# More row slots and a larger TensorE share for block 0's expert sum in a retention, attention and expert layer

## The chip, the cores and the metric

One core of a Trainium2 chip runs the whole layer. The metric is the device time of one execution in microseconds; the time before is 1657.94 us, the median of three runs (1656.93 to 1660.45).

## The reference

One decoder layer on 512 tokens of 1024 floats, all in fp32. The tokens are four blocks of 128.

```python
proj = x @ w_in                                     # 7 groups of 512 columns
r = silu(rg) * group_norm(retention(rot(rq), rot(rk), rv))     # 4 heads
d = 0.8 * rms_norm((softmax(q1 k1) - lam * softmax(q2 k2)) v)   # 4 heads, causal
x = layer_norm(alpha * x + concat(r, d) @ w_out)
q = x @ w_query                                     # 8 heads, 2 halves
# per head: 16 best keys of each half, 16 best of their 256 sums
idx, gate = top_pairs(q, sub_keys)                  # 128 experts for each token
h = gelu(sum_d(x * U[idx]))                         # one dot product per expert
ffn = sum_e(gate * h * V[idx])                      # one weighted row per expert
x = layer_norm(alpha * x + ffn)
```

Each token needs 128 rows of U and 128 rows of V, 4 KB each. These gathers are 537 MB of the 603 MB that the core moves.

## The kernel before, in words

**Block 0 goes first.** It is projected, mixed and queried alone (WAVES[0]), up to about 126 us. Then its 128 U rows and 128 V rows are gathered and used while blocks 1 to 3 are projected, mixed and queried (WAVES[1]). One gather fills one slot: the same expert position for all 128 tokens, 128x1024 floats, 512 KB. Four make a group, so there are 32 U groups and 32 V groups (`HALVES`). U group k is used by VectorE in `dots(k)` (L1039, second input in PSUM, result into `hid`). V groups are summed in two ways: groups 0 to 7 (`ON_PE`) by TensorE in `add_rows(j)` (L461), as a product with a diagonal matrix of the weights that ScalarE builds in `diagonals(j)` (L870), accumulated in the PSUM tile ACC; groups 8 to 31 by VectorE in `sums(k)` (L1052, both inputs and the output in SBUF).

**The slots.** `ring` has eight slots (arena columns 14K to 18K), two groups. The list `ROWS` gives the order of the 64 groups: U 0 to 19, then V and U in turn, then the rest of V. GpSimd (POOL) issues them in this order (L438); before each slot it waits until the group two places earlier in the list has been used (`slot_used`).

**The pairs.** For blocks 1 to 3, one gather brings an expert's U and V row together, 1 MB: 384 pairs (L426) into 18 slots (`fused`, `NS`). Three pairs are issued behind V group 21 and three behind group 24 (`early`); pair 6 and the rest stand behind all rows in POOL's queue, and pair 6 also waits until the queries' key scores are stored (`keys_scored`), since pair slots 6 to 13 hold the query's operands. Pairs 14 to 17 go into the memory of the eight row slots. Pair 18 and each after it wait until TensorE has summed the pair 18 places earlier (L474). VectorE makes the pairs' dot products (L1060).

**The order of the engines is written out by hand.** In blocks 1 to 3, `attend(b, beside)` on TensorE does for each head: the scores of the next head (L661), which wait for this head's exponentials; the V groups named in `beside`; the transposes of this head's probabilities (L681), which wait for VectorE's `softmax_join`; the product with v (L685), which waits for ScalarE's copy. ScalarE's `attention` does exponentials (L880, after the transposes of the head before), the diagonals of `beside`, then the copy (L888). VectorE does `softmax_max`, `rows(1)` (one group, U or V, whichever is next), `softmax_join`. After the four heads come ScalarE's squares (L896), VectorE's `diff_norm` (L1243), and on TensorE `mixed_out`: transposes (L707, L725) and the output projection (L716). VectorE's `ln1(b)` (from L1252) waits for the projection. `ln1(3)` is followed by the queries on TensorE (L744, scores L754), and by `retrieve` on VectorE, which ends with the expert numbers (L1311) that the pairs wait for.

**Weights.** A row's weight needs gelu of `hid`. ScalarE's `gelu_0` and VectorE's `weights` do it for quarters of 32 experts: quarter 0 ahead of block 1's heads, quarters 1 to 3 in block 3's head 0.

Of the kernel before, what the change touches and what calls it, by code (L numbers as in the profile page):

```python
# [29 lines left out]
ALU = mybir.AluOpType  # L30
# [23 lines left out]
RING = 8  # L54
HALF = RING // 2

# [8 lines left out]
AT = {row: p for p, row in enumerate(ROWS)}  # L65

# [54 lines left out]

def tiles_before(b):

    return b * (b + 1) // 2


def ring_slots(p):

    return range(p % 2 * HALF, (p % 2 + 1) * HALF)


def landed(p):

    return 16 * (p // 2 + 1)


def used(p):

    return p // 2 + 1
# [8 lines left out]
def build(nc, x, xT, w_in, ret_gn_g, ret_gn_b, lq1, lk1, lq2, lk2, subln_g, w_out, ln1_g, ln1_b,  # L148
          w_query, keysT, uv, ln2_g, ln2_b, decay, rope, ident_in, mask_in, decay_far, out):
    ctx = ExitStack()  # L150
    with ctx:
# [18 lines left out]
        dqT = part(2 * K + 1536, 1536, "p (h t) -> p h t", h=H)  # L170
        swish = part(2 * K + 3072, 1536, "p (i n) -> p i n", i=3)
        gn = part(2 * K + 4608, 1536, "p (i n) -> p i n", i=3)
        work = part(5 * K, D)
        dec = part(5 * K + D, D, "p (c n) -> p c n", c=2)
        attn = part(6 * K, 1536)
        rp = part(6 * K + 1536, 512, "p (c b n) -> p c b n", c=2, b=NB)
# [3 lines left out]
        ring = part(14 * K, 4 * K, "p (r d) -> p r d", r=RING)  # L180
# [10 lines left out]
        rv = sb("rv", [P, NB, HW])  # L191
        dkT = sb("dkT", [P, H, S])
# [207 lines left out]
        def _(pool):  # L400
# [4 lines left out]
            early = {("V", 21): (0, 3), ("V", 24): (3, EARLY)}  # L405
# [6 lines left out]
            def pair(n):  # L412
# [4 lines left out]
                if n == 0:  # L417
                    pool.wait_ge(mixer_ready, 2 * NB)
                elif n == EARLY:
                    pool.wait_ge(keys_scored, 4 + 3 * WQ)  # L420
                elif LATE <= n < NS:
                    for r in (2 * (n - LATE), 2 * (n - LATE) + 1):
                        pool.wait_ge(slot_used[r], HALVES)
                elif n >= NS:
                    pool.wait_ge(pairs_summed, n - NS + 1)
# [5 lines left out]
            for p, (table, k) in enumerate(ROWS):  # L431
                if table == "U" and k * HALF % QUARTER == 0:
                    pool.wait_ge(experts_ready, k * HALF // QUARTER + 1)
                for m, r in enumerate(ring_slots(p)):
                    if p >= 2:
                        pool.wait_ge(slot_used[r], used(p - 2))
                    e = k * HALF + m
                    pool.indirect_dma_start(  # L438
                        out=ring[:, r, :], out_offset=None, in_=rows,
# [8 lines left out]
        def _(pe):  # L448
            fill = [0]

            def add_rows(j):

                p = AT["V", j]
                for m, r in enumerate(ring_slots(p)):
                    e = j * HALF + m
                    if e == 0:
                        pe.wait_ge(ret_decayed, tiles_before(NB))
                    pe.wait_ge(row_landed[r], landed(p))
                    pe.wait_ge(diag_ready, e + 1)
                    for half in range(2):  # L460
                        last = nc.tensor.matmul(  # L461
                            ACC[:, half * HW:(half + 1) * HW], fdiag[:, e % ND, :], ring[:, r, half * HW:(half + 1) * HW],
                            start=e == 0, stop=e == ON_PE * HALF - 1)
# [305 lines left out]
            attend(1, [[0], [1], [2], [3]])  # L769
            add_rows(4)  # L770
            mixed_out(1)
            attend(2, [[5], [6], [7], []])
            mixed_out(2)
            attend(3, [[], [], [], []])
# [7 lines left out]
        def _(act):  # L782
# [74 lines left out]
            def project_1():  # L857

                for f in FILLS[fill[0]:]:
                    take_fill(1, WAVES[1])  # L860

            def diagonals(j):

                for e in range(j * HALF, (j + 1) * HALF):
                    if e == 0:
                        act.wait_ge(weights_ready, 1)
                    if e >= ND:
                        r, count = slot_of("V", e - ND)
                        act.wait_ge(slot_used[r], count)
                    nc.scalar.activation(fdiag[:, e % ND, :], ident[:], ACT.Copy,  # L870
                                         scale=gate[:, e:e + 1]).then_inc(diag_ready, 1)

            def attention(b, beside):
                keys_n = (b + 1) * P
                for h in range(H):
# [9 lines left out]
                    if b == 3 and h == 0:  # L885
                        gelu_0(1, 4, 2)
# [592 lines left out]
```

## Time and profile before

| | us |
|---|---|
| device time, median of three runs | 1657.94 |
| span of the profiled execution | 1633.5 |
| outside the span (their difference) | 24.4 |
| TensorE, VectorE busy in the span | 1276.5, 1155.6 |
| ScalarE, GpSimd busy in the span | 267.2, 625.2 |

The profiled execution has no time of its own beside its span, so the span is set against the median. The page gives busy shares over the whole span; the span has stages with different limits, so it is read by stretches, and then along the timeline of each engine.

### The profile page before, as it was taken

How to read it: one execution, taken by the hardware profiler on the slowest of the kernel's cores; microseconds unless marked ns; L12 is line 12 of the kernel's file. 1: busy time of each engine (PE TensorE's matmuls, PEld its weight loads, DVE VectorE, ACT ScalarE, POOL GpSimd, SP SyncE). 2: the span in 40 equal slices, each digit the busy share in tenths (PEclk: the TensorE clock that was granted, in tenths of full speed). 3: DMA queues.
4: the chain of work that ended last, by engine and by line, in shares of the span. 5: the costliest groups of instructions: out<-in, count | busy, mean ns of one | idle time of the engine just before them, and what ended most of it. 6: DMA issues, size and time to landing. Idle time of an engine off the chain costs nothing.

```text
span 1633.5 us, 11511 instructions
## 1 busy us (share of the span) xinstructions
PE 1276.5 (78%) x3448; PEld 618.1 (38%) x3448; DVE 1155.6 (71%) x2727; ACT 267.2 (16%) x754; POOL 625.2 (38%) x645
## 2 busy tenths in 40 slices
PE   7879979888646994586978687878777878787885
PEld 5465446433323562232323233333333333332332
DVE  1349999767798979987676767776767677764454
ACT  0110000121211111121212121212121212121111
POOL 0004344474445565543434343434342434343320
PEclk9989999999767997798888888989897989899899
DMA  9939798897759898999999999999999999999993
GB/s 339 390 140 353 280 344 312 319 409 274 263 189 335 319 373 329 410 422 421 422 421 421 422 422 421 422 421 422 421 422 421 422 421 422 421 422 421 421 422 127
DMA packets 125710, 603.44 MB, mean 369 GB/s; under 512 B 12624, under 2 KB 14928, under 8 KB 76368
## 3 DMA queue, kind: packets, MB, share of 16 engines
q0 software_dynamic: 92160, 536.91, 81.2%
q1 hardware_dynamic: 33488, 65.80, 11.0%
q8 instruction: 27, 0.44, 0.1%
q14 instruction: 35, 0.29, 0.1%
HBM read 600.57 MB, written 2.10 MB: 369 GB/s over the span
## 4 chain that ended last, share of the span: by engine, by line
DMA 38%; PE 31%; DVE 23%; issue 3%; POOL 2%; SPq 1%; ACT 1%; DVEq 0%; POOLq 0%
DMA arena<-uv,idx 37%; PE W L474 7%; PE W L509 7%; DVE arena L1060 5%; PE ACC L474 4%; DVE xs L1052 4%; PE W L744 3%; PE W L716 3%; PE ACC L461 2%; POOL arena L438 2%; PE W L515 2%; DVE arena L1039 1%; DMA arena<-w_in 1%; DVE cand L1301 1%; DVE cand L1303 1%
## 5 line engine op out<-in xcount | busy, mean ns | idle before, releaser
L474 PE MATMUL W<-arena,fdiag 128*128 128x512 f32 x1024 | 498.9, 648 | 170.1 <-ACT fdiag L979 170.1
L426 POOL DMA_INDIRECT arena<-uv,idx x384 | 367.5, 957 | 586.7 <-PE W L474 355.7
L1060 DVE SCALAR_TENSOR_TENSOR arena<-arena,X 128x1024 f32<-128x1024 f32 x256 | 309.2, 1219 | 200.8 <-DMA arena<-uv,idx 199.7
L438 POOL DMA_INDIRECT arena<-uv,idx x256 | 257.3, 1005 | 372.2 <-DVE idx L1311 125.1
L474 PEld LDWEIGHTS W<-arena,fdiag 128*128 128x128 f32 x1024 | 208.6, 208 | 459.7 <-issue 253.0
L474 PE MATMUL ACC<-arena,fdiag 128*128 128x512 f32 x512 | 254.9, 660 | 69.3 <-ACT fdiag L979 69.3
L1060 DVE SCALAR_TENSOR_TENSOR arena<-arena,W 128x1024 f32<-128x1024 f32 x128 | 154.8, 1219 | 95.8 <-DMA arena<-uv,idx 95.4
L474 PEld LDWEIGHTS ACC<-arena,fdiag 128*128 128x128 f32 x512 | 107.0, 213 | 217.2 <-issue 132.1
L979 ACT ACTIVATE fdiag<-ident,gate 128x128 f32<-128x128 f32 x384 | 123.3, 390 | 354.7 <-DVE gate L1067 351.0
L1039 DVE SCALAR_TENSOR_TENSOR arena<-arena,X 128x1024 f32<-128x1024 f32 x128 | 150.0, 1216 | 24.8 <-DMA arena<-uv,idx 24.3
L509 PE MATMUL W<-arena 128*128 128x512 f32 x320 | 143.7, 605 | 9.7 <-DMA arena<-w_in 9.0
L1052 DVE SCALAR_TENSOR_TENSOR xs<-arena,gate,xs 128x1024 f32<-128x1024 f32 x96 | 123.3, 1284 | 19.3 <-DMA arena<-uv,idx 11.1
L744 PE MATMUL W<-arena 128*128 128x128 f32 (+1 forms) x512 | 116.8, 391 | 1.4 <-ACT arena L912 1.4
L971 ACT ACTIVATE hid<-hid 128x4 f32<-128x4 f32 x96 | 19.7, 205 | 456.5 <-DVE arena L1060 456.5
L744 PEld LDWEIGHTS W<-arena 128*128 128x128 f32 x512 | 80.2, 198 | 36.2 <-ACT arena L912 2.2
L509 PEld LDWEIGHTS W<-arena 128*128 128x128 f32 x320 | 60.8, 194 | 81.9 <-issue 76.9
L515 PE MATMUL W<-arena 128*128 128x128 f32 (+1 forms) x256 | 58.9, 388 | 10.8 <-DVE arena L1157 9.4
L461 PE MATMUL ACC<-arena,fdiag 128*128 128x512 f32 x128 | 59.0, 615 | 4.2 <-DMA arena<-uv,idx 4.2
L515 PEld LDWEIGHTS W<-arena 128*128 128x128 f32 x256 | 39.0, 194 | 28.4 <-issue 11.8
L716 PE MATMUL W<-arena 128*128 128x512 f32 x96 | 43.8, 616 | 0.7 <-ACT arena L912 0.7
L461 PEld LDWEIGHTS ACC<-arena,fdiag 128*128 128x128 f32 x128 | 24.5, 197 | 36.0 <-issue 29.7
L716 PEld LDWEIGHTS W<-arena 128*128 128x128 f32 x96 | 18.7, 198 | 25.1 <-issue 23.2
(178 smaller groups left out, 824.7 us busy)
## 6 DMA issues: line engine op xcount, KB each, us to landing
arena<-w_in SPq DMA_DIRECT2D x13, 2048.0 KB, 13.8
arena<-peer_w_query SPq DMA_DIRECT2D x8, 2048.0 KB, 14.4
arena<-uv,idx POOLq DMA_INDIRECT x640, 25.4
arena<-w_out SPq DMA_DIRECT2D x4, 2048.0 KB, 14.9
arena<-w_in SPq DMA_DIRECT2D x4, 512.0 KB, 6.4
out<-xs SPq DMA_DIRECT2D x4, 512.0 KB, 8.1
arena<-xT SPq DMA_DIRECT2D x1, 1536.0 KB, 18.2
xs<-x SPq DMA_DIRECT2D x1, 1536.0 KB, 17.0
```

Source lines behind the costliest of these rows:

```text
L426: pool.indirect_dma_start(out=fused[slot], out_offset=None, in_=uv, in_offset=bass.IndirectOffsetOnAxis(ap=idx[:, E + n:E + n + 1], axis=0 ...
L438: pool.indirect_dma_start(out=ring[:, r, :], out_offset=None, in_=rows, in_offset=bass.IndirectOffsetOnAxis(ap=idx[:, e:e + 1], axis=0), e ...
L461: last = nc.tensor.matmul(ACC[:, half * HW:(half + 1) * HW], fdiag[:, e % ND, :], ring[:, r, half * HW:(half + 1) * HW], start=e == 0, sto ...
L474: last = nc.tensor.matmul(sum_of(b)[:, half * HW:(half + 1) * HW], fdiag[:, n % ND, :], fused[n % NS][:, D + half * HW:D + (half + 1) * HW ...
L509: last = nc.tensor.matmul(bank, actT[:, k, part * P:(part + 1) * P], wts[slot][:, k, :], start=(k == 0), stop=(k == KD - 1))
L515: last = nc.tensor.matmul(bank[:, at:at + n_tok], wts[slot][:, k, h * P:(h + 1) * P], actT[:, k, toks], start=(k == 0), stop=(k == KD - 1))
L716: last = nc.tensor.matmul(W[:, 2 + half, :], mixT[:, k, :], wts[slot][:, k, :], start=(k == 0), stop=(k == KD - 1))
L744: last = nc.tensor.matmul(dst, wts[slot][:, k, i * P:(i + 1) * P], actT[:, k, toks], start=(k == 0), stop=(k == KD - 1))
L979: nc.scalar.activation(fdiag[:, n % ND, :], ident[:], ACT.Copy, scale=gate[:, E + n:E + n + 1]).then_inc(pair_diag_ready, 1)
L1039: STT(out=ring[:, r, :], in0=ring[:, r, :], scalar=1.0, in1=X[:], op0=ALU.mult, op1=ALU.mult, accum_out=hid[:, e:e + 1]).then_inc(slot_use ...
L1052: STT(out=xs[:, 0, :], in0=ring[:, r, :], scalar=gate[:, e:e + 1], in1=xs[:, 0, :], op0=ALU.mult, op1=ALU.add).then_inc(slot_used[r], 1)
L1060: STT(out=fused[slot][:, 0:D], in0=fused[slot][:, 0:D], scalar=1.0, in1=token_of(b), op0=ALU.mult, op1=ALU.mult, accum_out=hid[:, E + n:E ...
```

## The change

There are sixteen row slots. The eight new ones lie in memory that is free once blocks 1 to 3's retention products are done (kT, rv, parts of the arena); `QUAD_AT` gives each group of `ROWS` four slots, two sets of four in turn up to U group 19, four sets in turn for the next 30 groups, two again from V group 18. POOL waits for `ret_mixed` before V group 0. TensorE sums 18 V groups (`PE_GROUPS`): 0 to 9, 11, 13, 15, 17 beside attention, and 28 to 31 after the queries of blocks 1 to 3. VectorE sums the other 14. The table `BESIDE` puts groups 3 and 4 into head 3 of block 1, 8 and 9 into head 3 of block 2, and one group into each head of block 3. The weights come in three steps: quarters 0 and 1 before the last projection, quarter 2 in block 2's head 2 with the scaling `residual(0)`, quarter 3 in block 3's head 0. VectorE's `rows` calls are set anew. Three early pairs each stand behind V groups 25 and 28, not 21 and 24. Pair 0 waits for the last use of slots 12 to 15, and ScalarE's first scores of blocks 1 to 3 for that of slots 8 to 11.

```diff
-RING = 8
-HALF = RING // 2
+RING = 16
+HALF = 4
 FIRST_V = 20
-ON_PE = 8
+AFTER_QUERY = [28, 29, 30, 31]
+PE_GROUPS = list(range(10)) + [11, 13, 15, 17] + AFTER_QUERY
+DVE_GROUPS = [j for j in range(HALVES) if j not in PE_GROUPS]
+TURNS = 10
 ROWS = ([("U", k) for k in range(FIRST_V)]
-        + [row for j in range(ON_PE) for row in (("V", j), ("U", FIRST_V + j))]
-        + [("U", k) for k in range(FIRST_V + ON_PE, HALVES)] + [("V", k) for k in range(ON_PE, HALVES)])
+        + [row for j in range(TURNS) for row in (("V", j), ("U", FIRST_V + j))]
+        + [("U", k) for k in range(FIRST_V + TURNS, HALVES)] + [("V", k) for k in range(TURNS, HALVES)])
+WIDE_FROM, WIDE_TO = FIRST_V, AT["V", 18]
+def quads_of(p):
+    if p < WIDE_FROM:
+        return p % 2
+    if p < WIDE_TO:
+        return ((p - WIDE_FROM) + 2) % 4
+    return (p - WIDE_TO) % 2
+WEIGH_AT = [None, (2, 2), (3, 0)]
+BESIDE = {1: [[0], [1], [2], [3, 4]], 2: [[5], [6], [7], [8, 9]], 3: [[11], [13], [15], [17]]}
+WEIGH = [(0, 2), (2, 3), (3, 4)]
...
-            early = {("V", 21): (0, 3), ("V", 24): (3, EARLY)}
+            early = {("V", 25): (0, 3), ("V", 28): (3, EARLY)}
...
+                if p == WIDE_FROM:
+                    pool.wait_ge(ret_mixed, NB)
                 for m, r in enumerate(ring_slots(p)):
-                    if p >= 2:
-                        pool.wait_ge(slot_used[r], used(p - 2))
+                    if used(p) > 1:
+                        pool.wait_ge(slot_used[r], used(p) - 1)
...
             query(1, WAVES[1])
+            for j in AFTER_QUERY:
+                add_rows(j)
             for b in range(1, NB):
                 add_pairs(b)
...
                 for f in FILLS[fill[0]:]:
+                    if fill[0] == len(FILLS) - 1:
+                        gelu_0(0)
                     take_fill(1, WAVES[1])
...
             gate_exp(4)
             gate_exp(5)
+            for j in AFTER_QUERY:
+                diagonals(j)
...
                     if h:
                         softmax_max(b, h)
-                    if taken[0] < HALVES or h:
-                        rows(1)
+                    rows(1)
                     softmax_join(b, h)
-                    if b == 2 and h == 0:
-                        rows(1)
                     if b > 1 and h == 0:
                         ln1(b - 1)
-                    if b == 3 and h == 0:
-                        weights(1, 4, 2)
+                    if (b, h) == WEIGH_AT[1]:
+                        weights(1)
                         residual(0)
+                    if (b, h) == WEIGH_AT[2]:
+                        weights(2)
+                    if b == 2 and h % 2:
+                        rows(1)
                 rows(1)
                 diff_norm(b)
                 if b < NB - 1:
                     softmax_max(b + 1, 0)
                 if b == 2:
-                    rows(HALVES - taken[0])
-            rows(3)
-            ln1(3)
-            rows(5)
-            retrieve(1, 0)
-            rows(5)
-            retrieve(1, 1)
-            rows(2 * HALVES - ON_PE - taken[0])
+                    rows(max(0, HALVES - taken[0]))
+            rows(2)
+            ln1(3)
+            rows(4)
+            retrieve(1, 0)
+            rows(3)
+            retrieve(1, 1)
+            rows(HALVES + len(DVE_GROUPS) - taken[0])
```

## Rows read from the trace of the kernel before

**Rows 1.** Page: span, engines' busy time, GB/s in 40 slices, dots of block 0

```profile
span 1633.5 us, 11511 instructions
...
PE 1276.5 (78%) x3448; PEld 618.1 (38%) x3448; DVE 1155.6 (71%) x2727; ACT 267.2 (16%) x754; POOL 625.2 (38%) x645
...
GB/s 339 390 140 353 280 344 312 319 409 274 263 189 335 319 373 329 410 422 421 422 421 421 422 422 421 422 421 422 421 422 421 422 421 422 421 422 421 421 422 127
...
L1039 DVE SCALAR_TENSOR_TENSOR arena<-arena,X 128x1024 f32<-128x1024 f32 x128 | 150.0, 1216 | 24.8 <-DMA arena<-uv,idx 24.3
```

**Rows 2.** Busy time by stretch: PE, PEld, DVE, ACT, POOL; PE clock, DMA share, GB/s

```profile
300.00:460.00 160.00, 125.40 (x355) 59.55 (x353) 110.73 (x252) 36.30 (x109) 79.34 (x84) 0.91 0.82 307
...
460.00:500.00 40.00, 14.29 (x47) 9.13 (x48) 37.60 (x61) 7.28 (x23) 20.14 (x16) 0.50 0.58 193
...
627.00:655.00 28.00, 2.53 (x23) 2.33 (x21) 25.91 (x21) 3.31 (x6) 21.90 (x21) 0.62 0.91 332
...
700.00:1590.00 890.00, 700.99 (x1422) 293.58 (x1421) 597.57 (x1441) 162.40 (x478) 334.94 (x353) 0.89 1.01 422
```

**Rows 3.** Timeline of POOL: start, duration, line, what, [idle before <- releaser]

```profile
316.59 0.94 POOL L438 DMA_INDIRECT arena<-uv,idx  x1 [17.46 <-DVE arena L1039]
...
319.07 0.94 POOL L438 DMA_INDIRECT arena<-uv,idx  x1 [0.30 <-issue]
...
386.97 0.93 POOL L438 DMA_INDIRECT arena<-uv,idx  x1 [0.78 <-PE ACC L461]
...
388.69 0.94 POOL L438 DMA_INDIRECT arena<-uv,idx  x1 [0.79 <-PE ACC L461]
...
571.73 1.73 POOL L426 DMA_INDIRECT arena<-uv,idx  x1 [14.77 <-DVE idx L1311]
...
626.38 1.93 POOL L438 DMA_INDIRECT arena<-uv,idx  x1 [15.12 <-DVE xs L1052]
...
628.62 1.08 POOL L438 DMA_INDIRECT arena<-uv,idx  x1 [0.30 <-issue]
...
655.00 1.08 POOL L426 DMA_INDIRECT arena<-uv,idx  x1 [0.30 <-issue]
```

**Rows 4.** Timeline of PE, 300 to 630 us: V rows, attention, output, queries

```profile
317.46 8.23 PE L461 MATMUL ACC<-arena,fdiag 128*128 128x512 f32 x16
...
348.39 7.13 PE L461 MATMUL ACC<-arena,fdiag 128*128 128x512 f32 x16 [1.70 <-DMA arena<-uv,idx]
...
365.60 1.04 PE L707 MATMUL W<-ident,arena 128*128 128x128 f32 x8
...
434.93 1.97 PE L707 MATMUL W<-ident,arena 128*128 128x128 f32 x8 [5.19 <-DVE arena L1243]
...
439.89 14.00 PE L716 MATMUL W<-arena 128*128 128x512 f32 x32
...
453.82 1.13 PE L661 MATMUL W<-dkT,arena 64*128 64x512 f32 x4
...
466.82 2.08 PE L661 MATMUL W<-dkT,arena 64*128 64x512 f32 x4 [9.06 <-ACT arena L880]
...
499.37 1.97 PE L707 MATMUL W<-ident,arena 128*128 128x128 f32 x8 [4.93 <-DVE arena L1243]
...
503.73 15.82 PE L716 MATMUL W<-arena 128*128 128x512 f32 x32 [0.69 <-ACT arena L912]
...
626.52 3.00 PE L754 MATMUL W<-arena 128*128 128x128 f32 x24 [0.58 <-ACT arena L929]
```

**Rows 5.** Timeline of DVE: the end of block 1's norm

```profile
360.87 1.13 DVE L1243 SCALAR_TENSOR_TENSOR arena<-W,rstd,arena 128x128 f32<-128x128 f32 x4
```

**Rows 6.** Timeline of ACT: table load and exponential in block 3, gates after the queries

```profile
456.57 1.28 ACT L880 ACT_TABLE_LOAD   x1
...
474.32 0.69 ACT L880 ACTIVATE arena<-W,nmax 128x512 f32<-128x512 f32 x1
...
630.06 0.34 ACT L965 ACTIVATE gate<-gate 128x32 f32<-128x32 f32 x2
```

More of the change, by code:

```diff
@@ L127, in ring_slots, with used, uses_of, weighed_by @@
 def ring_slots(p):
-    return range(p % 2 * HALF, (p % 2 + 1) * HALF)
+    return range(QUAD_AT[p] * HALF, (QUAD_AT[p] + 1) * HALF)
+def used(p):
+    return QUAD_AT[:p + 1].count(QUAD_AT[p])
 def landed(p):
-    return 16 * (p // 2 + 1)
-def used(p):
-    return p // 2 + 1
+    return 16 * used(p)
+def uses_of(quad):
+    return QUAD_AT.count(quad)
+WEIGH = [(0, 2), (2, 3), (3, 4)]
+def weighed_by(j):
+    return [n for n, (lo, hi) in enumerate(WEIGH) if lo <= j * HALF // QUARTER < hi][0] + 1
 def slot_of(table, e):
@@ L169, in build @@
         qT = part(2 * K, 1536, "p (h t) -> p h t", h=H)
[L170 to L176, printed above, removed]
+        rp = part(2 * K + 1536, 512, "p (c b n) -> p c b n", c=2, b=NB)
+        dqT = part(3 * K, 1536, "p (h t) -> p h t", h=H)
+        swish = part(3 * K + 1536, 1536, "p (i n) -> p i n", i=3)
+        work = part(3 * K + 3072, D)
+        dec = part(5 * K, D, "p (c n) -> p c n", c=2)
+        gn = part(5 * K + D, 1536, "p (i n) -> p i n", i=3)
+        attn = part(6 * K + 512, 1536)
         keys = part(7 * K, K, "p (c n) -> p c n", c=HC)
@@ L191, in build @@
         rv = sb("rv", [P, NB, HW])
+        kT_flat = kT[:].rearrange("p h n -> p (h n)")
+        rv_flat = rv[:].rearrange("p b n -> p (b n)")
+        ring = ([part(14 * K + r * D, D) for r in range(8)]
+                + [kT_flat[:, 0:D], kT_flat[:, D:2 * D], rv_flat[:, 0:D], rv_flat[:, D:2 * D]]
+                + [part(2 * K, D), part(2 * K + D, D), part(5 * K, D), part(D, D)])
         dkT = sb("dkT", [P, H, S])
@@ L418, in pair @@
                     pool.wait_ge(mixer_ready, 2 * NB)
+                    for r in range(12, RING):
+                        pool.wait_ge(slot_used[r], uses_of(3))
                 elif n == EARLY:
@@ L934, in query @@
                             act.wait_ge(keys_scored, m + 1)
+                            if w and s == 0 and j == 0:
+                                for r in range(8, 12):
+                                    act.wait_ge(slot_used[r], uses_of(2))
                             nc.scalar.activation(scores[b][:, s * HW:(s + 1) * HW], W[:, m % 2, :],
@@ L950, in token_to_psum, with gelu_0 @@
                 last.then_inc(token_in_psum, 1)
-            def gelu_0(lo, hi, call):
+            def gelu_0(call):
+                lo, hi = WEIGH[call]
                 cols = slice(lo * QUARTER, hi * QUARTER)
@@ L1075, in gate_norm, with weights @@
                 link(TT(out=g, in0=g, in1=gsum[:, 0:2].unsqueeze(2).to_broadcast([P, 2, TOPK]), op=ALU.mult))
-            def weights(lo, hi, calls):
+            def weights(call):
+                lo, hi = WEIGH[call]
+                calls = call + 1
                 cols = slice(lo * QUARTER, hi * QUARTER)
@@ L1118, in join_sums @@
                 if b == 0:
-                    for r, count in (slot_of("V", E - 1), slot_of("V", ON_PE * HALF - 1)):
+                    for r, count in (slot_of("V", DVE_GROUPS[-1] * HALF + HALF - 1),
+                                     slot_of("V", PE_GROUPS[-1] * HALF + HALF - 1)):
                         dve.wait_ge(slot_used[r], count)
@@ L1352, in rows @@
                     else:
-                        sums(k - HALVES + ON_PE)
+                        sums(DVE_GROUPS[k - HALVES])
                 taken[0] += n
@@ L1377, in _ @@
                 retention_norm(b)
-            weights(0, 1, 1)
+            weights(0)
             softmax_max(1, 0)
```

63 lines of the change are left out of this document (33 added, 30 removed).

## The prediction

> **What bounds the kernel now.** I read the page first: neither TensorE (78% busy) nor VectorE (71%) fills the span, but from slice 18 on the DMA moves 421 to 422 GB/s in every slice but the last [rows 1]. The table by stretch says the same: 422 GB/s from 700 to 1590 us, with VectorE busy 598 us of 890 [rows 2]. In that tail only bytes count. The timeline of POOL shows where it begins: pair 6 is issued at 655.00, and behind it all is determined by the 378 pairs left, so the span ends 978.5 us later (1633.5 - 655.0). **The question is thus when pair 6 is issued.** It needs two things: the queries of blocks 1 to 3 (TensorE's last key product ends at 626.52 + 3.00 = 629.5, which I call Q [rows 4]), and the 64 groups of block 0 ahead of it in POOL's queue.
>
> Before, it is the queue that is late. POOL stands 15.12 us, to 626.38, for a slot that VectorE frees only after its retrieval, then issues the last 20 rows, one each 1.39 us (1.08 + 0.30), and pair 6 follows at 655.0, 25.5 us after Q [rows 3]. The bytes in the stretches 300 to 460 (307 GB/s) and 460 to 500 (193 GB/s) show much idle DMA time, and 460 to 500 is VectorE's: busy 37.6 us of 40, TensorE only 14.3 [rows 2]. It is tempting to price the change by that idle DMA time. But bytes moved earlier shorten the span only if pair 6 comes earlier, and this has the floor Q.
>
> **The change, part by part.** (1) *The end of the queue.* At Q only V groups 30 and 31, 8 rows, remain ahead of pair 6: by list order pairs 3 to 5 and group 29 need only group 27's slots, which VectorE frees ahead of its second retrieval. Group 30 takes the slots of group 28, and 31 those of 29, and TensorE uses these after the queries. ScalarE's gate exponentials end 0.9 us after Q (630.06 + 0.34 [rows 6]); one diagonal later, about Q + 1.3, group 28 starts. A row on TensorE takes 1.72 us, as the spacing of POOL's issues shows where TensorE frees the slots (386.97 to 388.69 [rows 3]), so the first of the 8 issues comes near Q + 3.5, the eighth 7 x 1.72 = 12.0 later, and pair 6 one issue (1.24) behind, at Q + 16.8. For Q = 629.5 that is 646.3, or 8.7 us earlier. Bounds: 1.24 us per issue if the slots were free (Q + 13.4), and 2.06 if each row took what the slow group took (8.23 for four [rows 4]; Q + 19.2).
>
> What is queued behind these rows? On TensorE the pairs' sums: groups 28 to 31 hold it 4 x 6.9 = 27.6 us, to about Q + 29. Pair 18 needs pair 0's sum, at Q + 31. Pairs 6 to 17 are 12 MB, 30 us at 422 GB/s, so the DMA has work to Q + 47. Then TensorE needs 1.72 us per pair against the DMA's 2.49, and catches up. This costs nothing, with 16 us of cover. Nor do pairs 14 to 17 wait long for the slots of groups 30 and 31. VectorE has fewer rows (56 against 96 at 1.39, 55 us less), all of it ahead of Q or in slack.
>
> (2) *Q itself moves*, since TensorE now does 6 more groups inside the chain that leads to the queries. I walk this chain by blocks; shifts are against the trace.
> Block 1: weights 0 come before the last projection, so head 0 starts 1.1 us earlier (before, gelu, its table load and four small VectorE instructions stood there). The slots let V1 and U20 be fetched in the 17.46 us in which POOL stood [rows 3], so TensorE's wait of 1.70 for rows [rows 4] and one of 0.8 go. Against that, group 4 moves from behind the last head, where it covered the squares and the norm, to ahead of that head's transposes. Before: group 3 starts at 348.39 and L707 at 365.60. After: group 3 at about 345.3, two groups (13.8 to 14.0) to 359.3, then transposes, product, squares and norm, 6.6 us (348.39 + 7.13 = 355.5 to the norm's end at 360.87 + 1.13 = 362.0 [rows 5]), so L707 at 365.9: **+0.3**.
> Block 2: the second U group of head 1 (4 x 1.2 on VectorE [rows 1], then the next maximum) holds head 2's exponentials to 405.9; group 7 ends at 413.9; transposes and copy 1.0, a table load of 1.28, since gelu of quarter 2 now stands there (as in the row at 456.57 [rows 6]), exponentials and a diagonal 1.7, groups 8 and 9 14.0, and 6.9 as above: L707 at 438.8 against 434.93: **+3.9**.
> Block 3: L707 to the output projection as before (434.93 to 439.89, and 14.00 long), so the heads start at 457.7. Group 11 hides in the 9.06 us that TensorE waited [rows 4]; the table load that lay in that wait now follows it, and head 2's scores start at 470.1 against 466.82: +3.3. A head with a group is then a chain on TensorE and ScalarE: scores 1.13 [rows 4], rows 6.9, transposes and copy 1.2, two exponentials of 0.69 with what follows each 1.45 [rows 6], 0.1 to 0.3 between: 10.9 us, where VectorE alone had set 9.0. Two heads, then the last group, 7.0 and 7.2 for the rest: L707 at 506.3 against 499.37, **+6.9**. The last projection took 15.82 where it takes 14.00 at full clock [rows 4]; with a busier TensorE ahead of it I give back 1.4: **+5.5**. From there, norm, queries (about 100 us of TensorE without a gap over 1 us) and their scores are unchanged, so Q is 635.0. The row supply stays ahead of this: 4.97 us per group of issues against heads of 9 to 11 us that use two, with slots for four.
>
> (3) *Nothing or near it:* POOL's wait for `ret_mixed` (3 us late for V0, but V0 is used 17 us later), the waits for slots 8 to 15 (last used in block 3's heads, needed 50 us later), and the early pairs behind group 25, which stand from about 552 to 578 for the same retrieval that held them 14.77 us before [rows 3]; the DMA is idle there, but the floor Q isn't touched.
>
> Sum: pair 6 at 635.0 + 16.8 = 651.8, 3.2 us earlier; I take 3. Span 1630.5, and with the 24.4 us between the profiled span and the median of the runs **1655 us**.
>
> [...] While VectorE sums V rows, POOL's issues come each 1.39 us, with dots running each 1.24 (0.94 + 0.30) [rows 3]: the same step as VectorE's own instruction. [...]
>
> **The rivals.** A: *the groups fit in TensorE's waits, Q stays within 3 us of 629.5.* For: TensorE was 64% idle in 460 to 500 [rows 2]. Against: the waits are for VectorE in one head and the group must fit into each of them. Price: pair 6 at 646.3, 8.7 earlier, 1649.2 us; 0.22.
> B: *the added groups run at the lower clock, and it is slower.* In 460 to 500 the granted clock was 0.50, 1.2 GHz, and 64x512 scores took 2.08 against 1.13 [rows 2, 4]. Each of the four instructions per row then takes twice 0.43, a group 13.8. If so for groups 13, 15 and 17, Q moves 3 x 6.9 = 20.7 more, pair 6 comes at 672.5, 17.5 later: 1675.4. It decides from the first group that is slow (3.2 of gain against 6.9). Against: the clock was 0.91 over 300 to 460, where groups stood beside the heads, and groups there took 7.13. 0.10. The Trainium skill, TensorE: Matmul & The Clock Gate, on oscillation in real kernels, tells of kernels whose TensorE runs cold because each wait throttles it again, which would give B; the trace shows this for sparse heads and not for heads with groups.
> C: *the chain is longer than I walked it*, Q moves 8 to 14: a head waits for rows that fall together with the 2 MB weight loads, or diagonals and table loads add up. Pair 6 at 654.3 to 660.3: -0.7 to +5.3, 1657 to 1663; 0.18. The sixteen slots bring nothing then. Forecast, Q moves 3 to 8, -6 to -0.5: 0.50.
>
> **How the numbers follow.** 0.2%, 3.3 us, is about what a measurement can tell from no change. Faster: all of A and 0.22 of the forecast's case, 0.44. Same: 0.28 of it and 0.10 of C, 0.38. Slower: B and 0.08 of C, 0.18. The range goes from A less 2 us, 1647, over the bounds of Q + 13.4 to Q + 19.2, to C's end, 1663; beyond are B and an A with a shorter chain.
>
> **What would show it.** In the changed kernel: L707 of block 3 at 506 and L744 near 535 to 536; rows of V groups beside block 3's heads at 7 us with a granted clock near 1.0; the eight last row issues 1.72 apart, starting 3.5 us after the last L754; pair 6 near 652 and the span's end 978 later; 422 GB/s from there on without a dip near Q + 47. A Q below 632 shows A, groups of 13 us B. The prediction is wrong at its root if the span's end doesn't follow pair 6, for instance if TensorE's late start leaves pairs waiting.

## The result: 12 us slower, and the profile after

The changed kernel takes 1669.56 us (four executions, 1668.45 to 1671.28) where the kernel before takes 1657.43 beside it: the ratio is 1.0082, with a 95% interval of 1.0063 to 1.0101. The forecast was 3 us faster. These lines are from the page of the changed kernel; they answer [rows 1]. L1091 is now the dots of block 0, L503 `add_rows`, L479 POOL's row issues, L465 its pair issues, L749 and L758 `mixed_out` (transposes and projection), L1300 `diff_norm`.

```profile
span 1667.9 us, 11861 instructions
...
PE 1356.7 (81%) x3608; PEld 653.0 (39%) x3608; DVE 1104.6 (66%) x2691; ACT 282.7 (17%) x798; POOL 619.3 (37%) x645
...
GB/s 341 389 122 331 275 335 318 317 407 220 325 298 296 277 194 361 261 423 421 422 421 422 421 422 421 422 421 422 421 422 421 422 421 422 422 421 422 421 421 133
...
L503 PE MATMUL ACC<-arena,fdiag 128*128 128x512 f32 x208 | 95.0, 613 | 2.4 <-ACT fdiag L916 1.3
```

VectorE has 51 us less to do and TensorE 80 more, as planned, and from slice 17 on the DMA moves 421 to 423 GB/s again. So the loss lies before the tail. The end of POOL's row queue comes next; it answers [rows 3]. Columns here and in all timelines: start, duration, engine and line, what, [idle before <- releaser].

```profile
676.13 0.94 POOL L479 DMA_INDIRECT arena<-uv,idx  x1 [25.27 <-PE ACC L503]
677.85 0.94 POOL L479 DMA_INDIRECT arena<-uv,idx  x1 [0.78 <-PE ACC L503]
...
688.15 0.94 POOL L479 DMA_INDIRECT arena<-uv,idx  x1 [0.78 <-PE ACC L503]
689.39 0.94 POOL L465 DMA_INDIRECT arena<-uv,idx  x1 [0.30 <-issue]
```

And this is TensorE around Q, the end of the queries' last key product, in the same execution [rows 4]:

```profile
669.60 3.00 PE L796 MATMUL W<-arena 128*128 128x128 f32 x24 [0.58 <-ACT arena L977]
673.90 27.71 PE L503 MATMUL ACC<-arena,fdiag 128*128 128x512 f32 x64 [1.30 <-ACT fdiag L916]
```

Q is 672.6. The first of the eight last rows is issued 3.5 us later, they are 1.72 apart, pair 6 follows at 689.39, which is Q + 16.8, and the span ends 978.5 behind it (1667.9 - 689.39). The tail is thus as forecast, to the tenth. **The whole error is Q: 672.6, where 635.0 was forecast and 629.5 was before.**

Where does Q lose 43 us? The timelines of ScalarE and VectorE show something that the profile of before does not have. Lines of the changed kernel:

```profile
136.60 0.60 ACT L977 ACTIVATE arena<-W 128x512 f32<-128x512 f32 x1 [10.66 <-remote]
...
260.65 0.49 ACT L870 ACTIVATE arena<-W 128x384 f32<-128x384 f32 x1 [10.51 <-remote]
...
380.05 0.28 ACT L944 ACTIVATE arena<-W 128x128 f32<-128x128 f32 x1 [3.16 <-issue]
...
381.22 0.17 DVE L1297 TENSOR_SCALAR rstd<-ssq 128x4 f32<-128x4 f32 x1 [14.49 <-issue]
...
476.96 0.43 DVE L1260 TENSOR_TENSOR W<-W,mask 128x256 f32<-128x256 f32 x1 [10.80 <-remote]
```

In all five rows the profile finds no releaser and writes "issue" or "remote". That alone doesn't make a row late; the distance to what it needs does. At 380.05, ScalarE's squares start 3.11 us after the start of the product they read (376.94). In an execution without such gaps (e2 below) it is 0.75 (358.30 to 359.05). At 136.60 ScalarE has stood 10.66 us where it stands 6.55 in e2, so it is 4.1 late, and at 476.96 VectorE begins 6.3 us after the end of the scores that it needs (TensorE, 469.54 + 1.13). The row at 381.22 is not late itself: ScalarE's read of the last square in front of it ends at 381.19. I call the others **late starts**. Between 100 us and Q, 23 waits of over 0.8 us on ScalarE, VectorE and GpSimd have no releaser, 14 of them on ScalarE; they hold the ordinary waits too, so neither their number nor their length is the loss.

In three places two engines begin again almost together after such a wait: VectorE at 260.40 and ScalarE at 260.65, ScalarE at 476.90 and VectorE at 476.96 in this trace, ScalarE at 385.51 and GpSimd at 385.63 in that of e14. That looks like one cause for both, but no run shows it.

### The profile page after: what moved, and what is told of

Its sections match the earlier page's. It is cut to its first block, busy times and chain, and to the rows that moved or that the text cites. A ratio compares the mean times of both kernels' runs of the same rounds, so it can differ in the third digit from the quotient of the medians.

```text
span 1667.9 us, 11861 instructions
## 1 busy us (share of the span) xinstructions
PE 1356.7 (81%) x3608; PEld 653.0 (39%) x3608; DVE 1104.6 (66%) x2691; ACT 282.7 (17%) x798; POOL 619.3 (37%) x645
## 4 chain that ended last, share of the span: by engine, by line
PE 41%; DMA 37%; DVE 13%; issue 4%; ACT 2%; another core or an unknown queue 1%; SPq 1%; POOL 0%; POOLq 0%; DVEq 0%; ACTq 0%
DMA arena<-uv,idx 36%; PE W L516 7%; PE ACC L503 7%; PE W L786 7%; PE W L551 7%; PE ACC L516 3%; DVE arena L1114 3%; PE W L758 3%; PE W L557 2%; DVE arena L1091 1%; PE W L796 1%; DMA arena<-w_in 1%; PE W L629 1%; PE W L687 1%
## 5 line engine op out<-in xcount | busy, mean ns | idle before, releaser
L465 POOL DMA_INDIRECT arena<-uv,idx x384 | 368.3, 959 | 598.4 <-PE W L516 356.5
L1114 DVE SCALAR_TENSOR_TENSOR arena<-arena,X 128x1024 f32<-128x1024 f32 x256 | 309.8, 1220 | 210.2 <-DMA arena<-uv,idx 209.4
L479 POOL DMA_INDIRECT arena<-uv,idx x224 | 219.4, 979 | 379.2 <-DVE idx L1368 124.0
L516 PE MATMUL ACC<-arena,fdiag 128*128 128x512 f32 x512 | 253.9, 658 | 69.8 <-ACT fdiag L1031 69.8
L516 PEld LDWEIGHTS ACC<-arena,fdiag 128*128 128x128 f32 x512 | 106.7, 212 | 217.0 <-issue 131.8
L551 PE MATMUL W<-arena 128*128 128x512 f32 x320 | 145.6, 611 | 8.8 <-DMA arena<-w_in 8.1
L1091 DVE SCALAR_TENSOR_TENSOR arena<-arena,X 128x1024 f32<-128x1024 f32 x124 | 143.8, 1216 | 3.5 <-issue 2.2
L786 PE MATMUL W<-arena 128*128 128x128 f32 (+1 forms) x512 | 118.1, 394 | 1.7 <-ACT arena L960 1.4
L503 PE MATMUL ACC<-arena,fdiag 128*128 128x512 f32 x208 | 95.0, 613 | 2.4 <-ACT fdiag L916 1.3
L786 PEld LDWEIGHTS W<-arena 128*128 128x128 f32 x512 | 80.9, 200 | 36.6 <-issue 2.7
L551 PEld LDWEIGHTS W<-arena 128*128 128x128 f32 x320 | 61.6, 197 | 82.1 <-issue 78.2
L1106 DVE SCALAR_TENSOR_TENSOR xs<-arena,gate,xs 128x1024 f32<-128x1024 f32 x48 | 61.6, 1284 | 21.0 <-DMA arena<-uv,idx 17.4
L557 PE MATMUL W<-arena 128*128 128x128 f32 (+1 forms) x256 | 61.6, 400 | 8.3 <-DVE arena L1214 8.3
L503 PEld LDWEIGHTS ACC<-arena,fdiag 128*128 128x128 f32 x208 | 40.1, 196 | 55.0 <-issue 55.0
L758 PE MATMUL W<-arena 128*128 128x512 f32 x96 | 46.4, 645 | 7.6 <-ACT arena L960 7.6
L557 PEld LDWEIGHTS W<-arena 128*128 128x128 f32 x256 | 40.5, 200 | 26.8 <-issue 13.2
L758 PEld LDWEIGHTS W<-arena 128*128 128x128 f32 x96 | 19.6, 208 | 34.2 <-issue 25.4
## 6 DMA issues: line engine op xcount, KB each, us to landing
xs<-x SPq DMA_DIRECT2D x1, 1536.0 KB, 17.1
```

What stands on the lines that cost most here:

```text
L465: pool.indirect_dma_start(out=fused[slot], out_offset=None, in_=uv, in_offset=bass.IndirectOffsetOnAxis(ap=idx[:, E + n:E + n + 1], axis=0 ...
L479: pool.indirect_dma_start(out=ring[r], out_offset=None, in_=rows, in_offset=bass.IndirectOffsetOnAxis(ap=idx[:, e:e + 1], axis=0), element ...
L503: last = nc.tensor.matmul(ACC[:, half * HW:(half + 1) * HW], fdiag[:, i % ND, :], ring[r][:, half * HW:(half + 1) * HW], start=i == 0, sto ...
L516: last = nc.tensor.matmul(sum_of(b)[:, half * HW:(half + 1) * HW], fdiag[:, n % ND, :], fused[n % NS][:, D + half * HW:D + (half + 1) * HW ...
L551: last = nc.tensor.matmul(bank, actT[:, k, part * P:(part + 1) * P], wts[slot][:, k, :], start=(k == 0), stop=(k == KD - 1))
L557: last = nc.tensor.matmul(bank[:, at:at + n_tok], wts[slot][:, k, h * P:(h + 1) * P], actT[:, k, toks], start=(k == 0), stop=(k == KD - 1))
```

## The experiments

Each kernel was run beside the kernel before on the same chip; the chips are not all alike, and that is half of the answer. In the table, Q and pair 6 are from the profiled execution.

| run | us | before beside it | ratio (95%) | Q | pair 6 | late starts |
|---|---|---|---|---|---|---|
| before, the profile shown | | | | 629.5 | 655.0 | none |
| after, on record | 1669.6 | 1657.4 | 1.0082 (1.0063 to 1.0101) | 672.6 | 689.4 | yes |
| e1 before | 1636.3 | 1637.3 | 0.9995 (0.9981 to 1.0010) | 628.5 | 654.3 | none |
| e2 after | 1639.6 | 1637.3 | 1.0007 (0.9994 to 1.0020) | 640.5 | 657.3 | none |
| e3 | 1626.2 | 1637.3 | 0.9939 (0.9917 to 0.9961) | 639.1 | 643.4 | none |
| e4 | 1635.7 | 1637.3 | 0.9992 (0.9978 to 1.0006) | 639.3 | 656.1 | none |
| e5 | 1626.2 | 1638.6 | 0.9922 (0.9892 to 0.9951) | 630.8 | 647.6 | none |
| e6 | 1615.6 | 1638.6 | 0.9860 (0.9834 to 0.9886) | 627.9 | 632.3 | none |
| e7 | 1660.2 | 1638.6 | 1.0130 (1.0103 to 1.0158) | 661.5 | 678.3 | none |
| e8 after | 1639.6 | 1638.6 | 1.0010 (0.9994 to 1.0026) | 639.9 | 656.7 | none |
| e9 before | 1656.0 | 1654.4 | 1.0012 (0.9997 to 1.0027) | 646.0 | 671.4 | yes |
| e10 after | 1670.4 | 1654.4 | 1.0092 (1.0062 to 1.0122) | 671.5 | 688.3 | yes |
| e11 (= e6) | 1647.5 | 1654.4 | 0.9952 (0.9932 to 0.9972) | 661.8 | 665.2 | yes |
| e12 (= e7) | 1658.8 | 1639.0 | 1.0118 (1.0100 to 1.0137) | 662.8 | 679.6 | none |
| e13 (= e7) | 1673.6 | 1654.6 | 1.0104 (1.0073 to 1.0134) | 676.3 | 693.1 | yes |
| e14 | 1665.0 | 1654.6 | 1.0059 (1.0039 to 1.0078) | 666.2 | 683.0 | yes |

### e1 and e2: both kernels again, unchanged

> The kernel before, unchanged. In the changed kernel's trace the tail went as forecast (pair 6 at 689.39, 16.8 us after the queries' end Q at 672.6; the span ends 978.5 us after it), but Q lies 43.1 us later than in the trace of before, of which 14.4 us are there when block 1's attention begins, in code that the change hardly touches, beside gaps with no releaser in the program (issue, remote). Theory S: the trace of before was of an execution without such gaps, and its usual executions have them. Then this trace has a span near 1655, Q near 651, and gaps that sum up to some 20 us. Theory C: the gaps come with the change. Then this trace has the span 1633 to 1636, Q at 629 to 631, and no such gaps.

> The changed kernel, unchanged. Both theories: about 1669.5 us, 12 slower than before, Q near 672, pair 6 near 689. If the gaps (issue, remote) stand at the same instructions as in the first trace, they belong to the program; if at others, to the execution.

The kernel before takes 1637 here, by e1 and by the runs beside it, and its profile is the one shown ahead of the prediction (span 1633.6 against 1633.5). The changed kernel takes 1639.62, not the 1669 that I expected in both theories: 2.3 us more than before, within what can be told apart. In its trace no engine stands over 1.0 us without a releaser between 100 and 660 us. So the late starts do not come with the change (e9 below shows them in the kernel before), and 12 us slower became "the same". In the timed executions of these runs the device time is 1.7 to 3.0 us longer than the span, and mostly 1.8. So the "24.4 us outside the span" of the prediction is no time that a single execution spends outside its span: the profile of before came from an execution without late starts, and its three times (1656.93 to 1660.45) lie where before is with them (e9, 1656.0).

The trace of e2 is the one to set the forecast against, since both profiles are then free of late starts. TensorE, end of block 1:

```profile
350.58 3.60 PE L503 MATMUL ACC<-kT,fdiag 128*128 128x512 f32 x8
354.01 3.60 PE L503 MATMUL ACC<-rv,fdiag 128*128 128x512 f32 x8
357.44 0.38 PE L723 MATMUL W<-ident,arena 128*128 128x128 f32 x2
358.30 0.71 PE L727 MATMUL W<-arena 128*128 128x128 f32 x4 [0.47 <-ACT arena L936]
363.90 1.97 PE L749 MATMUL W<-ident,arena 128*128 128x128 f32 x8 [4.89 <-DVE arena L1300]
366.55 1.65 PE L703 MATMUL W<-dkT,arena 64*128 64x384 f32 x4 [0.69 <-ACT arena L952]
368.13 15.87 PE L758 MATMUL W<-arena 128*128 128x512 f32 x32
```

Group 4 now stands ahead of the head's transposes (L723) and product (L727), so TensorE has nothing to do while the squares and `diff_norm` are made: it stands 4.89 us. The transposes behind that wait take 1.97 where they took 1.04, and the projection 15.87 where it took 14.00 (365.60 to 382.22 before for both, 16.6 us; 363.90 to 384.00 now, 20.1). Blocks 2 and 3 have the same wait, 4.77 us each. The granted clock (the column behind the five busy times; the last is GB/s) says why, in e2:

```profile
351.00:359.00 8.00, 7.53 (x22) 3.47 (x20) 0.00 (x0) 0.38 (x1) 6.17 (x7) 1.00 1.03 410
364.00:368.00 4.00, 3.31 (x12) 1.97 (x12) 0.00 (x0) 1.19 (x2) 0.07 (x1) 0.50 1.02 409
368.00:372.00 4.00, 4.00 (x7) 1.81 (x6) 3.68 (x6) 2.09 (x8) 0.72 (x1) 0.51 1.01 404
372.00:384.00 12.00, 12.00 (x30) 5.04 (x29) 3.76 (x10) 0.31 (x2) 3.11 (x4) 1.00 0.54 183
```

It is 1.00 (2.4 GHz) ahead of the wait, 0.50 (1.2 GHz) for the transposes and the first 4 us of the projection, and 1.00 again after that.

How much such a wait costs is not the same in each execution. The last projection stands behind a wait of 4.8 to 4.9 us in both kernels; here it is in e1 and in e2:

```profile
503.50 14.00 PE L716 MATMUL W<-arena 128*128 128x512 f32 x32 [0.69 <-ACT arena L912]
...
513.71 16.47 PE L758 MATMUL W<-arena 128*128 128x512 f32 x32 [0.69 <-ACT arena L960]
```

It took 15.82 in the profile of before and 14.00 in e1, which is the same kernel, and 16.47, 16.55 and 14.00 in e2, e8 and e3. So up to 2.5 us of a single trace's Q are chance. Block 1's projection, behind its new wait, is slow in all of e2, e3, e4 and e8 (15.2 to 16.3).

### e3 and e4: the last 16 rows, and block 3's heads

> Changed kernel, but V groups 28 to 31 are summed by VectorE behind its second retrieval and not by TensorE behind the queries. Theory T (the last rows wait for TensorE after the queries and cost 15 us there): rows 30 and 31 are issued before Q, pair 6 at Q + 1 to Q + 3 in place of Q + 16.8, so 13 to 15 us faster than the changed kernel: 1654 to 1657. Rival: VectorE is as late as in the kernel before (25.5 us after Q) and nothing is gained or it is slower: 1669 to 1678.

```diff
-AFTER_QUERY = [28, 29, 30, 31]
+AFTER_QUERY = []
```

13.5 us faster than e2, as expected, with Q as good as unchanged (639.1): pair 6 is issued 4.3 us after Q (Q + 1 to Q + 3 was expected) and not 16.8, as TensorE's four groups are no longer ahead of it. **The part of the change that puts 16 rows behind the queries costs 12.5 us of path**, even though the forecast counted its end, Q + 16.8, as a gain over Q + 25.5. Both are true: against the old order it is better, against VectorE doing the same rows in the new order it is worse.

> Changed kernel, but V groups 11, 13, 15, 17 are summed by VectorE, so that block 3's heads have no rows on TensorE. Theory W (the rows beside block 3's heads lengthen the chain): Q comes 5 to 8 us earlier; VectorE has 22 us more to do, behind its second retrieval, which may hold groups 28 and 29 to about Q: 1662 to 1668. Rival G (Q is late because of gaps of no releaser, not of rows): Q moves by less than 3 us or at random, 1668 to 1675.

```diff
-PE_GROUPS = list(range(10)) + [11, 13, 15, 17] + AFTER_QUERY
-BESIDE = {1: [[0], [1], [2], [3, 4]], 2: [[5], [6], [7], [8, 9]], 3: [[11], [13], [15], [17]]}
+PE_GROUPS = list(range(10)) + AFTER_QUERY
+BESIDE = {1: [[0], [1], [2], [3, 4]], 2: [[5], [6], [7], [8, 9]], 3: [[], [], [], []]}
```

Four groups less beside block 3's heads move Q by 1.2 and the time by 3.9. Theory W, which took the whole shift of 6.9 for block 3's, misses. Rival G has the size right, but not the reason, as there are no late starts here. Q alone misleads, though. The transposes behind the norms of blocks 2 and 3 in e4:

```profile
444.42 1.97 PE L749 MATMUL W<-ident,arena 128*128 128x128 f32 x8 [4.78 <-DVE arena L1300]
...
508.22 1.97 PE L749 MATMUL W<-ident,arena 128*128 128x128 f32 x8 [4.94 <-DVE arena L1300]
```

From one to the other it is 63.8 us, and 67.1 in e2 (442.29 to 509.35): the four groups cost 3.3 us of the path. The walk had put 3.0 there (the shift grows from 3.9 to 6.9), so this step held. The traces differ by nearly as much ahead of it: e4 reaches block 2's transposes 2.1 later than e2, with the same program up to there. Without the groups the last projection is no faster (16.43 against 16.47).

### e5 and e6: the last group moved behind the head

> Changed kernel, but in each of blocks 1 to 3 the last V group (4, 9, 17) stands behind the last head's product, beside squares and norm, as group 4 did before the change. In the changed kernel's trace on the chip of the last runs TensorE waits 4.8 to 4.9 us for the norm in each block, and after it the transposes take 1.97 in place of 1.04, the first projection 15.87 in place of 14.00, the last 16.47. Theory N (the uncovered norm and the lower clock behind it carry most of Q's shift of 11 us): three times 4.8 and some 4 us of clock, Q 12 to 18 us earlier, pair 6 still at Q + 16.8, so 12 to 18 us faster than the changed kernel beside it and 0.989 to 0.994 of the kernel before. Rival H (the heads' own length carries it): the group's 7 us come back elsewhere, less than 4 us faster.

```diff
-BESIDE = {1: [[0], [1], [2], [3, 4]], 2: [[5], [6], [7], [8, 9]], 3: [[11], [13], [15], [17]]}
+BESIDE = {1: [[0], [1], [2], [3]], 2: [[5], [6], [7], [8]], 3: [[11], [13], [15], []]}
+BEHIND = {1: 4, 2: 9, 3: 17}
...
+            add_rows(BEHIND[b])      # TensorE, behind attend(b)
...
+            diagonals(BEHIND[b])     # ScalarE, behind attention(b)
```

13.4 us faster than e2 and e8 (ratio to before 0.9922). The same stretch of TensorE as above, in e5 (L504 is `add_rows`, L750 and L759 `mixed_out`):

```profile
353.24 0.71 PE L728 MATMUL W<-arena 128*128 128x128 f32 x4 [0.47 <-ACT arena L940]
355.57 3.67 PE L504 MATMUL ACC<-kT,fdiag 128*128 128x512 f32 x8 [1.61 <-ACT fdiag L920]
359.07 3.60 PE L504 MATMUL ACC<-rv,fdiag 128*128 128x512 f32 x8
362.51 1.04 PE L750 MATMUL W<-ident,arena 128*128 128x128 f32 x8
364.28 0.92 PE L704 MATMUL W<-dkT,arena 64*128 64x384 f32 x4 [0.74 <-ACT arena L956]
365.13 14.00 PE L759 MATMUL W<-arena 128*128 128x512 f32 x32
```

The same two half-groups now lie in the wait; the transposes follow without a gap at 1.04 us, the projection takes 14.00. Its end is 379.13, 4.9 earlier, in block 1 alone. Q is 630.8, 9.1 to 9.7 earlier, with the same groups on the same engines. So what a group costs depends on its place. By the ends of the projections, blocks 1 and 2 give 4.9 and 4.7 us and block 3 nothing (379.13, 451.90, 521.73 against 384.00, 461.50, 530.18). There head 3 has no group now, TensorE stands more ahead of group 17, and that one runs in part at the lower clock (0.50 from 495 to 499):

```profile
495.12 10.02 PE L504 MATMUL ACC<-arena,fdiag 128*128 128x512 f32 x16 [1.61 <-ACT fdiag L920]
```

The 13.4 us are between medians; the profiled executions are 10.4 apart (1638.34 and 1627.94), which is the path.

> As the last one, and V groups 28 to 31 on VectorE, behind its second retrieval, as in e3 (which was 13 us faster than the changed kernel). If the two parts are independent the gains add: 25 to 31 us faster than the changed kernel, 0.981 to 0.986 of before. If VectorE becomes the one that is late (in e3 pair 6 came 4.3 us after Q, with row issues that waited for VectorE), only 17 to 24 us.

Both edits together: 1615.58, ratio 0.986 (0.9834 to 0.9886), the best version. The sum of the two alone would be 26.9 below e2, it is 24.0. At pair 6 nothing of the sum is missing: e3 and e5 move it by 13.9 and 9.7 us against e2, e6 by 25.0. In e6, as in e3, the tail behind it is 2 us longer than in e2 (981.1 and 980.9 against 979.1); why is open. POOL's timeline of e6:

```profile
620.35 1.93 POOL L480 DMA_INDIRECT arena<-uv,idx  x1 [15.06 <-DVE xs L1113]
622.58 1.09 POOL L480 DMA_INDIRECT arena<-uv,idx  x1 [0.30 <-issue]
...
632.30 1.09 POOL L466 DMA_INDIRECT arena<-uv,idx  x1 [0.30 <-issue]
```

With Q at 627.9 it is again the queue that is late, by VectorE's retrieval, the picture of [rows 3] with 8 rows behind it in place of 20.

### e7 and e12: only eight slots

> Changed kernel with the division of work and the order of the rows as changed, but only eight row slots in use; the two waits for the last use of slots 8 to 15 go, since these are not used. Theory R (the slots are what lets the rows keep ahead): heads wait for rows, Q 8 to 30 us later. Rival: the slots bring nothing, since a head of 9 to 11 us uses two groups and their issue takes 9.9: within 4 us of the changed kernel.

```diff
 def quads_of(p):
-    if p < WIDE_FROM:
-        return p % 2
-    if p < WIDE_TO:
-        return ((p - WIDE_FROM) + 2) % 4
-    return (p - WIDE_TO) % 2
+    return p % 2
```

(with the waits for the last use of slots 8 to 15 gone as well). 20.6 us slower than e8, Q 21.6 later. TensorE's timeline of e7, same stretch, `add_rows` at L497:

```profile
335.48 10.19 PE L497 MATMUL ACC<-arena,fdiag 128*128 128x512 f32 x16 [1.48 <-DMA arena<-uv,idx]
...
359.04 8.66 PE L497 MATMUL ACC<-arena,fdiag 128*128 128x512 f32 x16 [4.28 <-DMA arena<-uv,idx]
```

TensorE waits for rows in front of a group, and behind such waits the groups take 10.19 and 8.66 us in place of 7.13, at the lower clock (0.50 from 335.5 to 339 us, 0.61 from 359 to 363). With this division of the sum the sixteen slots are what carries it.

> Changed kernel with eight row slots in use, to be read on a chip where the late starts occur (before at 1650 to 1660 beside it). There the queries' end Q was 17.4 us later in the kernel before (628.5 to 646.0), but 31.6 us later in the changed one (639.9 to 671.5) and 33.9 in the variant with groups behind the heads. Theory D (twice as many row transfers in flight make the late starts more or longer): with eight slots Q goes from 661.5 on a quiet chip to 675 to 682, by 14 to 20. Rival K (the chain through ScalarE has less cover, whatever the slots): by 28 to 36, Q at 690 to 697. On a quiet chip (before at 1633 to 1641) both give Q 661 and 1660 us, and it tells nothing.

This one was meant for a chip with late starts and met one without: the time is that of e7.

### e8 to e11 and e13: the same kernels where engines start late

> The changed kernel once more, beside these. On the chip of the last runs it was 2.3 us slower than before (1639.6 against 1637.3) and had no gaps without a releaser; in the first measurement, 12.1 us slower (1669.6 against 1657.4), ScalarE started late at some ten places, 1 to 6 us each. If these gaps come from the chip and not from the run, this one gives about 1639 and a trace without gaps if it is on that chip, or 1665 to 1672 with gaps, and before at 1655 to 1660, if it is on one like the first.

A second chip without late starts: 1639.60, as e2.

> The kernel before, unchanged, to catch the condition of the first measurement (before 1657.4, changed 1669.6), whose changed trace has about 32 us of late starts of ScalarE with no releaser in the program. Theory P (the condition is one of the place where a kernel runs and delays every program): if it holds here, before is at 1655 to 1660 and its trace has such gaps of some 20 us in sum ahead of pair 6; if not, 1633 to 1640 without gaps.

> The changed kernel beside it. Under the condition: 1666 to 1672 with 25 to 35 us of gaps, since its chain leaves ScalarE less cover; without it 1637 to 1641, no gaps.

Here before takes 1656.0 and after 1670.4, ratio 1.0092: the result on record is there again. In e9 the kernel **before** has late starts too, the first in the same place as the changed kernel's:

```profile
136.94 0.60 ACT L929 ACTIVATE arena<-W 128x512 f32<-128x512 f32 x1 [10.59 <-remote]
```

So the condition is no property of the changed kernel alone. But its price is: before, Q moves from 628.5 to 646.0 (+17.4), after, from 639.9 to 671.5 (+31.6).

> The variant with the last group of a block behind its heads and groups 28 to 31 on VectorE. Without the condition 1614 to 1617, 0.986 of before, as before. Under it: pair 6 in this variant waits for the queries and for VectorE's rows, so 20 to 30 us of gaps on ScalarE move it by as much: 1636 to 1646, still faster than before beside it.

The best version loses 33.9 at Q (627.9 to 661.8) and 31.9 of time, and is still ahead of before, 0.9952 (0.9932 to 0.9972).

> As e12, which fell on a quiet chip. Where the late starts occur (before at 1650 to 1660 beside it), theory D (more transfers in flight make the late starts): Q from 661.5 to 675 to 682; rival K (less cover on the chain): Q at 690 to 697. Quiet: 661 and 1660 us, no answer.

The changed kernel with eight slots loses 13.5 to 14.8 at Q (661.5 and 662.8 to 676.3, where theory D expected 675 to 682 and rival K 690 to 697) and 14 of time, by one trace and two executions. The surplus of some 14 us over the kernel before (31.6 - 17.4) thus goes with the sixteen slots, and not with the new order or the larger share of TensorE, which e13 has as well. Without late starts the slots gain 20.6 (e7 against e8), with them only 3.2 (e13 against e10, on two chips), which the intervals of the two ratios don't tell from nothing.

### e14: one block's norm covered, with late starts

> Changed kernel, but V group 4 alone stands behind block 1's last head, beside squares and norm; blocks 2 and 3 as changed. In the changed kernel the wait for this norm is 4.9 us, and from the transposes to the projection's end it takes 20.1 us against 16.6 before, at the lower clock. If wait and clock are both given back: 7 to 9 us faster than the changed kernel. If only the wait: 4 to 5. If the rest of the chain absorbs it: under 2.

```diff
-BESIDE = {1: [[0], [1], [2], [3, 4]], 2: [[5], [6], [7], [8, 9]], 3: [[11], [13], [15], [17]]}
+BESIDE = {1: [[0], [1], [2], [3]], 2: [[5], [6], [7], [8, 9]], 3: [[11], [13], [15], [17]]}
...
+            add_rows(4)              # TensorE, behind attend(1)
...
+            diagonals(4)             # ScalarE, behind attention(1)
```

5.4 us faster than e10 (on another chip, with before at 1654.6 and 1654.4 beside them), Q 5.3 earlier, between the two sizes expected. TensorE in e14:

```profile
378.81 1.04 PE L749 MATMUL W<-ident,arena 128*128 128x128 f32 x8
386.65 1.65 PE L703 MATMUL W<-dkT,arena 64*128 64x384 f32 x4 [6.81 <-ACT arena L953]
```

The wait for the norm is gone and L749 comes 6.4 earlier than in e10 (378.81 against 385.22), but then ScalarE's copy is late, TensorE stands 6.81, and the scores run at 1.65 again. Covering one wait doesn't remove the late starts, they turn up at the next dependence.

## Why the prediction failed, by its own steps

**The end of the queue (step 1) held.** Q + 3.5, seven steps of 1.72 and Q + 16.8 are as forecast in e2 (640.5, 644.00, 657.26) and on record. The 978.5 from there to the end came out exactly on record and as 979.1 in e2; over all traces it is 978.4 to 982.4. The pairs behind the four groups cost nothing: `add_rows` took 27.71 of the forecast 27.6, and the DMA did not dip behind it.

**The walk to Q (step 2) was too short by half, without any late start.** It gave +5.5, e2 shows +11.0 against the 629.5 it started from (+11.9 against e1). Point by point, forecast and e2: first L707 (now L749) 365.9 and 363.9, second 438.8 and 442.3, third 506.3 and 509.35, end of the last projection 525.1 (506.3 + 20.2 - 1.4) and 530.2. The waits for the norm were in the walk (6.6 to 6.9 per block); what it left out is **what such a wait does to the clock behind it**. Block 1's transposes and projection take 20.1 where I kept 16.6, +3.5. I had assumed in the last block that a busier TensorE would give back 1.4 of the 15.82 of [rows 4], and it took 16.47: with the rest of that stretch +2.1. Block 2's heads took 2.0 more than walked, and that is the clock too: behind a wait of 2.53 us group 7 took 9.23 in place of 7.13, at clock 0.50 from 408 to 412. The other terms are within 0.8 and block 1 was 2.0 better than walked. These sum to the 5.5 that are missing (3.5 + 2.1 + 2.0 - 2.0 and small terms). Only the first is in each trace of this order; the 2.1 are 0 in e3, and block 1's gain is chance in part (its transposes begin at 362.6 in e8 and 367.2 in e3, with the same program up to there). The rows were there to be read: in [rows 4] L707 takes 1.04 in block 1, behind groups, and 1.97 in block 3, behind a wait of 4.93, with 15.82 for the projection after it. The change puts block 1 into that case, and I kept its 1.04 and 14.00. (Block 2 is no counterexample: its projection takes 14.00 in both kernels, since the transposes of x and the scores stand between and take the slow stretch.) In rival B I had asked whether the clock would slow the added groups; groups 13, 15 and 17 took about 7.1 each in e2, and it was group 7 and the product behind the norm that were slowed. The Trainium skill, TensorE: Matmul & The Clock Gate, section HAM oscillation — how this bites in real kernels, describes this for a wait on a DMA: the wait lets the clock down, and the products that follow pay for it. The trace agrees for a wait on VectorE: 15.87 us, with clock 0.51 in the first 4 us, behind the wait, 14.00 and 1.00 without it (e2, e5).

With the true Q, step 3's sum would have been pair 6 at 640.5 + 16.8 = 657.3, 2.3 later than before, and that is what e2 measured (+2.3 us, not clear of noise): rival C's case, to which I gave 0.18.

**The conversion to device time was wrong.** I took 1657.94 - 1633.5 = 24.4 us as lying outside the span; it is about 2 (1.7 to 3.0). That number was the sign that profile and times came from different conditions. Forecast faster or slower didn't depend on it as long as both kernels lose the same, which leads to the last point.

**The sign on record was decided by a term the prediction did not have.** Late starts add 17.1 us to the kernel before (1637.3 to 1654.4) and 30.8 to the changed one (1639.6 to 1670.4). 2.3 + 30.8 - 17.1 = 16.0, the distance of e10 to the kernel before; on record it is 12.1, with before at 1657.4. Against the forecast it adds up so: the span on record is 37.4 us longer than forecast (1667.9 against 1630.5), 5.5 by the walk and 32.1 by late starts (Q of 672.6 against e2's 640.5). The device time is only 14.6 longer (1669.6 against 1655), as 24.4 us had been added where 1.8 belonged. That two large errors cancelled in part is luck. That this surplus goes with the sixteen slots is what e13 and e7 show. How it comes about is argued only: with the slots, TensorE's and ScalarE's steps follow each other with less wait for rows in between, so a late start is less often hidden in one. The number of transfers in flight could also make each late start longer; no run separates the two. What makes an engine start late at all is open. Places come again (136.60 and 136.94 in two kernels, the block times of after on record and of e10 agree within 1.1 us), and by the times of before it is the chip that decides: 1650.7 to 1661.4 in all its executions on two chips, 1632.4 to 1644.0 in all on three others.

**What was right beside that:** the slots matter only through Q, bytes moved early shorten nothing (from 460 to 500 us the DMA of e2 moves 310 GB/s where before it moved 193 [rows 2], and the time is the same). VectorE's smaller share (51 us less busy) was off the path: e3 gives it 16 rows back and is faster. That the waits for slots 8 to 15 and for `ret_mixed` cost nothing is not tested, as no run leaves out these alone.

## What to carry to other kernels

When work is moved to another engine, ask where in its chain it lies relative to the waits it used to fill: one group per block, in front of a head and not behind it, cost 9 to 10 us of the path to Q and 10 of the profiled span (13 between medians), with the same work done by the same engines. A wait on TensorE is to be priced with the slower products behind it, read from the same instruction behind a wait and without one, in more than one trace, since the same 32 products behind the same wait took 14.00 to 16.55. And before a profile is used to the microsecond, its span should be set against the timed runs: a gap of 24 us where others show 2 means that the profile doesn't show the condition in which the times are taken.

## What the hardware showed that I had not expected

Late starts: on some chips an instruction begins up to 6 us after its last dependence (2.4 at 380.05 of the changed kernel, 6.1 in e14's row at 386.65, against 0.74 in e5), several of them at the same places from run to run and with no releaser in the trace, on ScalarE, VectorE and GpSimd. They cost 17 us of 1637 in one kernel, 31 to 32 in two with sixteen row slots, 13 to 15 in the changed kernel cut to eight. A change of 20 us on one chip (the slots, e7 against e8) is one of 3 us on another. Two kernels can therefore be compared only beside each other on one chip, and a ratio found on one need not hold on the next: 1.0007 and 1.0010 for this change on two chips, 1.0082 and 1.0092 on record and on a third.
